# Issuing the attention scores of two key/value heads in turn in a hybrid decoder layer

## What is computed

```
proj = h @ W_in                       # q_a: 8 heads x 64, k_a and v_a: 2 heads x 64
s = q k^T / 8 + bias                  # query head 4g+t uses key/value head g
s = where(0 <= i - j < 128, s, -inf)  # a block of 128 queries sees its own and the previous block
m = max(max(s), sink)                 # a sink logit for each head
p = exp(s - m) / (sum(exp(s - m)) + exp(sink - m))
attn = p @ v
mix = concat(attn, gla) @ W_out
```

## Time and profile before

| | |
|---|---|
| median of 3 runs | 1211.66 us |
| lowest and highest | 1210.81 and 1213.51 us |
| profiled execution, span from first to last instruction | 1207.3 us |
| stage over blocks, from the first L650 to the end of its last turn | 238.45 to 377.10 us of the span |

### The profile page before, as it was taken

How to read it: one execution, slowest core, us unless ns; L and a number is a source line. 1 busy time by engine, 2 the same in 40 slices (tenths; PEclk the granted TensorE clock), 3 DMA queues, 4 the chain that set the end, 5 groups by cost and what they waited for, 6 DMA issues and landing times.

```text
span 1207.3 us, 15516 instructions
## 1 busy us (share of the span) xinstructions
PE 1145.6 (95%) x6115; PEld 957.5 (79%) x6115; DVE 566.5 (47%) x887; ACT 376.7 (31%) x717; POOL 63.7 (5%) x72
## 2 busy tenths in 40 slices
PE   1799999999998999899999999999999999999995
PEld 1678868977786999688888888888888888888884
DVE  6657556687776423713332332422422423424436
ACT  1630101467666104544214113213114123023023
POOL 0002110021221000000000000000000000000001
PEclk9989999999999999799999999999999999999998
DMA  9838540100004511021212121121111211211103
GB/s 359 244 97 300 196 140 1 36 1 1 1 1 144 136 35 36 1 70 35 70 35 66 40 64 43 35 70 35 52 55 35 70 35 35 70 36 35 53 1 139
DMA packets 60746, 87.83 MB, mean 73 GB/s; under 512 B 13987, under 2 KB 43148, under 8 KB 60684
## 3 DMA queue, kind: packets, MB, share of 16 engines
q1 hardware_dynamic: 55916, 70.09, 18.3%
q0 software_dynamic: 4768, 16.82, 4.0%
HBM read 82.69 MB, written 4.21 MB: 72 GB/s over the span
## 4 chain that ended last, share of the span: by engine, by line
PE 91%; DVE 3%; ACT 2%; DMA 1%; SPq 1%; issue 0%; POOL 0%; ACTq 0%
PE bank L499 40%; PE bank L474 38%; PE bank L688 4%; PE bank L653 2%; DMA x_in<-in_x 1%; PE bank L629 1%; PE bank L618 1%; PE bank L569 1%; DVE act_lo L887 1%; PE bank L713 1%; PE bank L537 0%; SPq L302 0%; DVE act_full L885 0%; PE bank L664 0%; SPq L293 0%; DVE x L1245 0%
## 5 line engine op out<-in xcount | busy, mean ns | idle before, releaser
L474 PE MATMUL bank<-act_hi,w_hi 128*128 128x512 f32 x672 | 264.9, 394 | 0.4 <-issue 0.4
L474 PE MATMUL bank<-act_lo,w_hi 128*128 128x512 f32 x672 | 263.6, 392 | 0.0
L474 PE MATMUL bank<-act_hi,w_lo 128*128 128x512 f32 x672 | 263.3, 392 | 0.0
L1280 ACT ACTIVATE w_hi<-raw 128x2048 fp32r<-128x2048 f32 x45 | 86.2, 1915 | 464.2 <-PE bank L499 229.0
L499 PE MATMUL bank<-w_hi,hid_hi 128*128 128x512 f32 x512 | 199.2, 389 | 0.0
L499 PE MATMUL bank<-w_lo,hid_hi 128*128 128x512 f32 x512 | 199.2, 389 | 0.0
L499 PE MATMUL bank<-w_hi,hid_lo 128*128 128x512 f32 x512 | 199.2, 389 | 0.0
L1162 DVE TENSOR_TENSOR hid_lo<-bank,hid_hi 128x512 fp32r<-128x512 f32 x64 | 44.2, 690 | 238.7 <-ACT hid_hi L1470 238.7
L1190 DVE TENSOR_TENSOR x<-bank,x 128x512 f32<-128x512 f32 x120 | 81.1, 689 | 154.0 <-PE bank L499 153.5
L474 PEld LDWEIGHTS bank<-act_hi,w_hi 128*128 128x128 f32 x672 | 127.7, 190 | 27.4 <-issue 0.9
L474 PEld LDWEIGHTS bank<-act_lo,w_hi 128*128 128x128 f32 x672 | 127.5, 190 | 26.7 <-issue 0.2
(11 more groups left out here) (173 smaller groups left out, 1240.1 us busy)
## 6 DMA issues: line engine op xcount, KB each, us to landing
ada_w<-in_w_ada POOLq DMA_DIRECT2D x32, 512.0 KB, 6.8
raw<-in_w_mlp_in SPq DMA_DIRECT2D x64, 256.0 KB, 3.4
raw<-in_w_mlp_out SPq DMA_DIRECT2D x64, 256.0 KB, 3.4
raw<-in_w_in SPq DMA_DIRECT2D x36, 256.0 KB, 5.0
ada_w_first<-in_w_ada SPq DMA_DIRECT2D x8, 1024.0 KB, 10.4
x_in<-in_x SPq DMA_DIRECT2D x8, 512.0 KB, 15.5
raw<-in_w_out SPq DMA_DIRECT2D x16, 256.0 KB, 4.4
x<-in_x SPq DMA_DIRECT2D x8, 512.0 KB, 4.3
```

Source lines behind the costliest of these rows:

```text
L474: mm = pe.matmul(bank[2 * half + m][:, :], w, act(b)[:, k, half * HALF:half * HALF + HALF], start=(n == 0), stop=(n == 3 * KT - 1))
L1280: a.activation(w_hi[:, par, :], raw[:, par, :], ACT.Copy).then_inc(s_hi, 1)
```

## The change

`front` takes a half r (query heads 2r and 2r+1 of both key/value heads) in place of a key/value head g. Its four matmuls alternate between key/value head 0 (partitions 0 to 63, bank 0) and 1 (partitions 64 to 127, bank 1). It waits once, for both banks, ahead of its first matmul. The halves of the softmax are regrouped with it: slots of `prob` now hold heads 0, 1, 4, 5 in the first half and 2, 3, 6, 7 in the second. So the bias and the sinks are put down in another order (`PAIR_OF`), and `attend` takes its 512 columns as two runs of 256 out of the two halves of `prob_t`. VectorE's and ScalarE's loops keep every line.

```
-                                       prob_t[:, g, kb, :], start=(kb == 0), stop=(kb == 1))
+                                       prob_t[:, :, kb, 2 * g * P:2 * (g + 1) * P], start=(kb == 0), stop=(kb == 1))
...
-            def front(n, g, first=False):
-
-                for hp in (2 * g, 2 * g + 1):
-                    if not first or hp >= 2:
-                        pe.wait_ge(s_sc_free, 4 * n + hp - 1)
-                    for j in range(2):
-                        h = 2 * hp + j
-                        t = h % 4
-                        q = q_t[g * DH:(g + 1) * DH, t, tok(n)]
+            def front(n, r, first=False):
+
+                if not first or r > 0:
+                    pe.wait_ge(s_sc_free, 4 * n + 2 * r)
+                for j in range(2):
+                    for g in range(HEADS // 4):
+                        q = q_t[g * DH:(g + 1) * DH, 2 * r + j, tok(n)]
                         if first:
-                            mm = pe.matmul(bank[hp % 2][:, j * 256 + P:j * 256 + 256], q,
+                            mm = pe.matmul(bank[g][:, j * 256 + P:j * 256 + 256], q,
                                            k_t[g * DH:(g + 1) * DH, P:2 * P], start=True, stop=True)
                         else:
-                            mm = pe.matmul(bank[hp % 2][:, j * 256:j * 256 + 256], q,
+                            mm = pe.matmul(bank[g][:, j * 256:j * 256 + 256], q,
                                            k_t[g * DH:(g + 1) * DH, n * P:(n + 2) * P], start=True, stop=True)
-                    mm.then_inc(s_sc_full, 1)
+                        if j == 1:
+                            mm.then_inc(s_sc_full, 1)
...
+PAIR_OF = (0, 2, 1, 3)
...
-            v.tensor_scalar(n_sink, n_sink, -1.0, None, ALU.mult)
+            for i in range(HEADS // 2):
+                pair = PAIR_OF[i]
+                v.tensor_scalar(n_sink[:, 2 * pair:2 * pair + 2], sinks[:, 2 * i:2 * i + 2], -1.0, None, ALU.mult)
...
             for i in range(4):
-                ins = a.activation(bias[:, 2 * i:2 * i + 2, :], bank[4 + i][:, :].rearrange("p (h k) -> p h k", h=2),
+                pair = PAIR_OF[i]
+                ins = a.activation(bias[:, 2 * pair:2 * pair + 2, :],
+                                   bank[4 + i][:, :].rearrange("p (h k) -> p h k", h=2),
                                    ACT.Copy)
```

More of the change, by code:

```diff
@@ L215, in build @@
     b_col = vec(6 * KT)
+    sinks = vec(HEADS)
     n_sink = vec(HEADS)
@@ L328, in _ @@
             sp.dma_start(rev[:, :], reversal).then_inc(s_const, 16)
-            sp.dma_start(n_sink, attn_sinks[0:1, :].broadcast_to([P, HEADS])).then_inc(s_sink, 16)
+            sp.dma_start(sinks, attn_sinks[0:1, :].broadcast_to([P, HEADS])).then_inc(s_sink, 16)
             with nc.allow_non_contiguous_dma(reason="256 gate biases, one a partition"):
```

## The result

The changed kernel takes 1204.22 us (median of 4 runs, 1202.46 to 1205.40) against 1211.62 for the kernel before in the same runs: a ratio of 0.9934 with a 95% interval of 0.9917 to 0.9951. It is faster by 7.4 us; 1204.3 was forecast.

What follows compares the result with a forecast made beforehand. A ring of waits between TensorE and VectorE, not TensorE alone, was taken to set each turn; block 0's 0.16, turn 1's 1.07 and 6 x 1.02 gave 7.35 us, from 1211.66 to 1204.3, range 1202 to 1207.

Steps and rivals of the forecast that it cites:

- A front: Score matmuls of one front on TensorE: halves of the rows overlap, four steps of 0.215 us go, 1.92 to 1.06.
- A turn: One turn of the stage over blocks: 17.82 us becomes 16.80, so 1.02 saved, though TensorE alone would save 1.72.
- The ring: Chain of waits between TensorE and VectorE around one turn: 1.06 + 1.13 + 8.58 + wait 0.05 + 5.98 = 16.80 us.
- TensorE's slack: At L637, ahead of the transposes of the GLA output: TensorE will wait some 0.70 us a turn for VectorE.
- The second ring: Chain by way of L1062: VectorE's stretch 13.96, then 0.05, 0.59, 1.06 and 1.13, 16.79 us in all, a tie.
- The tightened wait: front(n, 1) now needs both L1026 and starts 0.04 us late; costed at nothing, being within the 0.70 of slack.
- Turn 1 and block 0: Start of the stage: turn 1 goes from 17.94 to 16.87 us, saving 1.07; block 0 saves 0.16, between 0 and 0.9.
- The sum: Whole run: 0.16 + 1.07 + 6 x 1.02 = 7.35 us saved, median from 1211.66 to 1204.3; chance 0.77.
- TensorE throughout: Rival: TensorE sets the pace throughout, 7 x 1.72 + 0.9 = 12.9 us saved, run 1198.8; chance 0.06.
- No overlap: Rival: the matmul pairs in a front do not run side by side, run 1211.7 us; chance 0.04.
- GpSimd ahead: Rival: GpSimd's L442 gets ahead of VectorE's fourth L1043 and holds it up, run 1214.4 or 1217.8 us; chance 0.08.
- Slow reads: Rival: attend reads its two runs of 256 columns slowly, at twice its 1.94 us, run 1213.0; chance 0.05.

## Why the prediction was right, and where it was not

**A front.** Right: 1.06 forecast, 1.06 measured, and 1.14 from its first start to its last modelled end against 1.99. L664's order carried over to 256 columns.

**A turn.** Right: 16.80 forecast and measured. The ring held in every part; the wait at L637 cost 0.05, as taken (296.10 to 296.15). TensorE's slack there was a little under the 0.70 forecast. The start of `gla_scores` in turn 3, before and after:

```profile
299.09 0.71 PE L664 MATMUL bank<-gq_t,gk_t 64*128 64x128 f32 x8
...
294.88 0.72 PE L667 MATMUL bank<-gq_t,gk_t 64*128 64x128 f32 x8
```

Before, 0.65 passed from there to L637 (299.74), so L641 could have come at 295.53 and came 0.62 later. The price agrees: of 1.18 added to the second front 0.55 showed, and 0.63 was hidden.

The second ring did not tie. VectorE's stretch took 13.85 in place of 13.96, so that ring is some 0.1 shorter than the turn: L727's part that needs L1067 began 0.17 after it (301.39 to 301.56), not 0.05. It also explains VectorE's idle time of 2.94, where about 2.85 was named. What made the stretch shorter was not traced.

**The tightened wait.** It cost nothing on the path, as forecast: the second front starts 2.48 after the transposes (288.88 - 286.40), and 2.43 before (292.25 - 289.82). The 0.05 came out of the slack.

**Turn 1 and block 0.** This step failed. 0.16 and 1.07 were to be saved; in the profile the two together went from 31.62 to 32.09. Two things were missed.

One is the half clock, a term that the forecast did not have. The run without the Newton step has the same block 0 and the same gap, and kept its clock:

```profile
252.22 0.65 PE L727 MATMUL bank<-state_b,gq_t 64*64 64x128 f32 x8 [2.23 <-DVE state_b L1067]
252.22:252.80 0.58, 0.58 (x9) 0.41 (x9) 0.58 (x1) 0.00 (x0) 0.58 (x1) 1.00 0.00 0
```

There block 0 took 252.80 - 239.07 = 13.73, where the changed kernel took 14.19; with the 1.10 by which turn 1 exceeds 16.80 the half clock cost 1.56 us in this execution. Without it the two would take 30.53, against 30.39 forecast.

The other is VectorE beside GpSimd in block 0. First the operation of VectorE in the kernel before, then the changed kernel:

```profile
249.69 1.28 DVE L805 SCALAR_TENSOR_TENSOR raw<-raw,small,gate 128x1024 f32<-128x1024 f32 x1
...
247.40 1.63 DVE L808 SCALAR_TENSOR_TENSOR raw<-raw,small,gate 128x1024 f32<-128x1024 f32 x1
249.47 1.17 DVE L1045 TENSOR_TENSOR small<-small 128x4 f32<-128x4 f32 x1
...
247.01 2.26 POOL L446 TENSOR_SCALAR g_low<-g_copy 128x512 f32<-128x512 f32 x1 [12.53 <-ACT g_copy L1411]
249.36 1.26 POOL L449 TENSOR_TENSOR silu_g<-silu_g,g_low 128x512 f32<-128x512 f32 x1
```

The idle 0.16 went, but L808 took 1.63 next to L446, and so L1067 came no earlier (12.50 after the first score matmul, 12.44 before). What TensorE saved in block 0 only made its wait for L1067 longer.

**The sum.** 6 x 1.02 came out as 6 x 1.02 (17.82 - 16.80 each). The stage as a whole gave 5.70 of the 7.35 in the profiled execution, and it would have given 7.26 without the half clock. That the median moved by 7.4, as forecast, is thus partly luck; how much of it cannot be said, for the other runs have no profile that shows whether they had the half clock. The 4.3 by which the median before stood above its profile was not what lies around a span either: runs of that kernel with the span on record have 2.2 there (1211.84 for 1209.6), the changed kernel 2.05 (1203.35 for 1201.3). The profiled execution before was thus some 2.1 better than its median.

**The rivals.** TensorE throughout: no, by the runs with one front in series and the run without the Newton step. No overlap: no, a front takes 1.06. GpSimd ahead: its L446 did move closer, from 1.03 after the first L1043 began to 0.88 after the first L1048, but the four L1048 kept their 1.14; if anything it is GpSimd that was held up, L446 taking 2.04 where L442 took 1.92. The lead of VectorE's fourth operation was more than the 0.01 forecast: narrow windows have it start at 303.96 before (0.24 ahead of L442) and at 300.53 now (0.09 ahead of L446). That VectorE loses where GpSimd comes first is seen in block 0, where one L1045 took 1.17 beside L449 (0.15 in a turn); in a turn it was not tried. Slow reads: L633 takes 1.94 as before; two runs of 256 columns cost nothing.

**The limit behind the matmuls.** The Trainium skill, TensorEngine Tiling (Array Packing), section Performance Considerations, warns that emptying PSUM does not get faster with tiling. The traces agree that VectorE comes next. But of VectorE's 8.56 us only two pairs of L1031, 2.57 us, read score banks. Another 1.73 reads GLA results out of PSUM (L1082 0.60, L1092 1.13), which the change does not touch; the rest is softmax and GLA work in SBUF and waits.

## What to carry to other kernels

Before a stage of the busiest engine is shortened, write down the ring: which engine waits for which, once around a turn, until the parts add up to the measured turn. Its smallest term says how much of a saving will get through in which place. Here it was the 0.21 us between VectorE's release and TensorE's arrival: what the first front saved came through whole, and of what the second saved only 0.16. When a saving has opened a gap, look for work of the next turn that neither engine needs until later, and put it there: this gave another 6.6 us after the 7.4 of the change itself.

## What the runs showed of the hardware that was not expected

- Matmuls on different halves of the rows need not alternate in the program. Four records of one half ahead of four of the other ran side by side all the same: 1.14 us for eight in either order.
- A front straight behind matmuls of its own form (`gla_scores`, 64*128 in the rows) takes 0.96; behind ones of another form it takes 1.06, be it 64*64 (L727) or 128*128 (L622). With one head group after the other it is 1.82 against 1.92 (301.75 - 299.93 in the kernel before with the early front). So a change of form costs about 0.1 us, an estimate from these four.
- The same gap of 2.2 us on TensorE at the end of block 0 was followed by a granted clock of 0.50 in four profiles (the changed kernel, heads one after the other, and the two with a front in series) and not in a fifth (without the Newton step). A second gap, of 2.27 or 2.28 us, stands in the tail of all ten profiles; TensorE's `attend` behind it took 1.94 at 1.00 in five of them and 3.26 to 3.54 at 0.53 to 0.57 in the other five. Gaps of 1.15, 1.16 and 1.81 in block 0 were not followed by it. At the end of block 0 the half clock cost 1.56 us in the changed kernel. So the length of the gap alone does not say whether the clock falls; what does is not shown by these runs.
- Next to GpSimd a very short operation of VectorE lost as much as a longer one: in block 0 L1045, on 128x4 elements, took 1.17 us beside L449 (0.15 in a turn). In the kernel before, one L1043 on 128x256 elements took 1.43 there (0.35 in a turn).
